# Two causal attentions of a two-block network on one core: the mask written into PSUM by ScalarE instead of added by TensorE

## What is computed

```python
# fox_attention, per block of 128 queries
logits = einsum('bhqd,bhkd->bhqk', qh[:, :, s0:end], kh[:, :, :end])
logits = logits + c[:, :, s0:end, None] - c[:, :, None, :end]
mask = (s0 + arange(Q_BLOCK))[:, None] >= arange(end)[None, :]
p = softmax(where(mask, logits, -inf), axis=-1)
outs.append(einsum('bhqk,bhkd->bhqd', p, vh[:, :, :end]))

# mla_mixer, per block of 128 queries
s = einsum('bqhd,bkhd->bhqk', qn, k_nope) + einsum('bqhr,bkr->bhqk', qp, k_pe)
s = where(k_idx[None, :] <= q_idx[:, None], s * scale, NEG_INF)
p = softmax(s, axis=-1)
```

## Time and profile before

| | before |
|---|---|
| median of three runs | 2364.09 us (2361.83 to 2372.06) |
| profiled execution, its own time | 2368.16 us |
| its span | 2366.2 us |
| PE busy | 2260.8 us (96%), 29050 instructions |
| PEld busy | 2018.5 us (85%) |
| DVE busy | 597.1 us (25%) |
| ACT busy | 474.1 us (20%), 1038 instructions |
| POOL busy | 40.9 us (2%) |
| granted TensorE clock, mean | 0.983 |
| DMA | 522.04 MB, mean 221 GB/s |
| stretch of the fox attention | about 526 to 569 us |
| stretch of the MLA attention | about 923 to 960 us |

### The profile page before, as it was taken

The page is one execution under the profiler, slowest core; times in us unless marked ns, Lnnn a source line. Parts: engine busy times, 40 slices in busy tenths (PEclk is TensorE's granted clock), DMA queues, the critical chain, the costliest instruction groups (busy, mean ns, idle before and its releaser), DMA issues.

```text
span 2366.2 us, 64576 instructions
## 1 busy us (share of the span) xinstructions
PE 2260.8 (96%) x29050; PEld 2018.5 (85%) x29050; DVE 597.1 (25%) x1485; ACT 474.1 (20%) x1038; POOL 40.9 (2%) x31
## 2 busy tenths in 40 slices
PE   7998999899899989999997899999999999999998
PEld 6877888667788866788885789999999999999998
DVE  3414332204333235311359320111111111111111
ACT  3422111213221124201123121111111111111111
POOL 0000000000000000000014100000000000000000
PEclk9999999999999999999998999999999999999999
DMA  7122443140333313233431239999999999999996
GB/s 310 72 116 97 160 160 142 72 159 26 147 138 142 140 66 148 107 115 152 195 125 37 107 130 352 382 354 379 356 387 350 383 345 391 333 396 339 397 357 260
DMA packets 103107, 522.04 MB, mean 221 GB/s; under 512 B 8369, under 2 KB 8498, under 8 KB 95410
## 3 DMA queue, kind: packets, MB, share of 16 engines
q1 hardware_dynamic: 102962, 519.82, 57.3%
HBM read 518.74 MB, written 1.05 MB: 220 GB/s over the span
## 4 chain that ended last, share of the span: by engine, by line
PE 91%; DVE 6%; ACT 1%; issue 1%; DMA 0%; SPq 0%; DVEq 0%; ACTq 0%
PE ps L1479 25%; PE ps L957 18%; PE ps L1493 13%; PE ps L936 10%; PE ps L968 9%; PE ps L1014 3%; PE ps L918 2%; PE ps L1180 1%; PE ps L1466 1%; DVE scr L1971 1%; PE ps L982 1%; PE ps L1437 1%; DVE rstd L1596 1%; PE ps L1123 1%; PE ps L1166 1%
## 5 line engine op out<-in xcount | busy, mean ns | idle before, releaser
L1479 PE MATMUL ps<-scr,slot 128*64 128x96 f32 x14336 | 636.4, 246 | 3.7 <-issue 3.7
L1479 PEld LDWEIGHTS ps<-scr,slot 128*64 128x64 f32 x14336 | 611.3, 137 | 4.6 <-issue 4.6
L957 PE MATMUL ps<-hT,slot 128*128 128x256 f32 x2016 | 445.4, 379 | 0.0
L957 PEld LDWEIGHTS ps<-hT,slot 128*128 128x128 f32 x2016 | 383.0, 190 | 52.1
L1493 PE MATMUL ps<-scr,slot 128*64 128x96 f32 x7168 | 341.4, 247 | 0.2 <-issue 0.2
L1493 PEld LDWEIGHTS ps<-scr,slot 128*64 128x64 f32 x7168 | 313.5, 137 | 24.4 <-issue 24.3
L968 PE MATMUL ps<-scr,slot 128*128 128x256 f32 x1056 | 242.3, 383 | 4.9 <-DVE scr L1806 4.9
L968 PEld LDWEIGHTS ps<-scr,slot 128*128 128x128 f32 x1056 | 202.7, 192 | 34.5 <-DVE scr L1806 6.5
L814 ACT ACTIVATE scr<-ps 128x96 f32<-128x96 f32 x224 | 56.2, 251 | 826.3 <-PE ps L1479 826.3
L2100 DVE TENSOR_TENSOR scr<-scr,ps 128x96 f32<-128x96 f32 x224 | 56.4, 252 | 613.2 <-PE ps L1479 613.2
L936 PE MATMUL ps<-hT,slot 128*128 128x256 f32 x736 | 166.1, 385 | 3.5 <-DVE hT L1583 2.9
(11 more groups left out here) (333 smaller groups left out, 1428.6 us busy)
## 6 DMA issues: line engine op xcount, KB each, us to landing
slot<-in_w_moe SPq DMA_DIRECT2D x224, 1024.0 KB, 7.1
slot<-in_w_moe SPq DMA_DIRECT2D x224, 512.0 KB, 6.9
slot<-in_w_ffn SPq DMA_DIRECT2D x33, 3072.0 KB, 10.1
slot<-in_w_even_in SPq DMA_DIRECT2D x4, 3072.0 KB, 23.0
slot<-in_w_odd_qk SPq DMA_DIRECT2D x2, 3072.0 KB, 10.1
slot<-in_w_s_glu SPq DMA_DIRECT2D x2, 3072.0 KB, 10.6
slot<-in_w_odd_v SPq DMA_DIRECT2D x2, 2048.0 KB, 8.4
slot<-in_w_even_out SPq DMA_DIRECT2D x1, 3072.0 KB, 10.1
```

The source lines that it names most:

```text
L957: m = pe.matmul(pair(f, k), w[:, o:o + P], hT[:, c], start=c == 0, stop=c == KD - 1, skip_group_check=True)
L1479: m = pe.matmul(pair(f, k)[s:s + STRIP, 0:CAP], w[:, o:o + STRIP], xg[e % 2][:, c], start=c == 0, stop=c == KD - 1, skip_group_check=True)
```

## The change

The mask no longer goes onto the scores behind them, but lies in PSUM ahead of them, and the products add onto it.

- GpSimd builds mask3 in SBUF, 384 columns wide: mask, zeros, mask. It does so once, when mixT of the first layer is complete (parts 22 and 23 of the scratch tensor; mag_ moves from there to part 11).
- For pairs 0 and 1 of each attention TensorE writes mask3 into the two banks by one product with the identity per head (start=True), ahead of the head products.
- For pairs 2 to 7 ScalarE copies mask3 into the bank of each head, in biased(p), behind turned(p) and ahead of mixed(p-1); it waits for the exponents of pair p, which read these banks last. TensorE's scores(p+2) waits for biased(p) in place of the exponents.
- All products of scores now have start=False. The mask products behind them are gone, and at["scores"] is incremented by the last product of each head (L1204 in fox, the second L1235 of a head in MLA).

The diff, without the list of semaphores:

```diff
@@ -325,7 +325,8 @@
         mraw = part(0, 6).rearrange("p (a n) -> p a n", a=6)
         mnorm = part(6, 5).rearrange("p (a n) -> p a n", a=5)
         qpe_raw = part(12, 4).rearrange("p (a n) -> p a n", a=4)
-        kpe, cos, sin, ang, turns, red, mag_ = (part(16 + i) for i in range(7))
+        kpe, cos, sin, ang, turns, red, mag_ = (part(i) for i in (16, 17, 18, 19, 20, 21, 11))
+        mask3 = part(22, 2)[:, 0:3 * P]
         posf = scr[0:1, 24 * T:25 * T]
         onesrow = scr[0:1, 25 * T:25 * T + P]
         tmp = part(30, 2).rearrange("p (a n) -> p a n", a=2)
@@ -455,6 +456,10 @@
             pool.affine_select(out=sc, in_=sc, pattern=[[0, 16], [1, CHUNK]], base=0,
                                channel_multiplier=-1, compare_op=ALU.is_ge, fill=0.0
                                ).then_inc(hg["masked"], 1)
+            pool.wait_ge(mix_ready, KD)
+            for b in (0, 2):
+                pool.tensor_copy(mask3[:, b * P:(b + 1) * P], mask).then_inc(at["maskmade"], 1)
+            pool.memset(mask3[:, P:2 * P], 0.0).then_inc(at["maskmade"], 1)
 
             def phase(q):
 
@@ -604,6 +609,13 @@
                                    bias=stat[:, h, 4:5], scale=scale_of[kind],
                                    accum_out=stat[:, h, 6:7]).then_inc(at["exp"], 1)
 
+                def biased(p):
+
+                    act.wait_ge(at["exp"], n0 + 2 * p + 2)
+                    for h in (2 * p, 2 * p + 1):
+                        act.activation(ps[:, 4 + h % 4, 0:3 * P], mask3, ACT.Copy
+                                       ).then_inc(at["biased"], 1)
+
                 def turned(p):
 
                     act.wait_ge(at["pturned"], n0 + 2 * p + 1)
@@ -616,6 +628,7 @@
                     act.wait_ge(at["out"], p0 + p + 1)
                     act.activation(mixT[:, p], ps[:, p % 2, 0:T], ACT.Copy).then_inc(mix_ready, 1)
 
+                act.wait_ge(at["maskmade"], 3)
                 exponents(0)
                 exponents(1)
                 for p in range(HEADS // 2):
@@ -623,6 +636,8 @@
                         exponents(2 * p + 2)
                         exponents(2 * p + 3)
                     turned(p)
+                    if p + 2 < HEADS // 2:
+                        biased(p)
                     if p:
                         mixed(p - 1)
                 mixed(HEADS // 2 - 1)
@@ -1111,18 +1126,18 @@
             def attention(kind, products):
                 n0 = at0[kind]
                 p0 = n0 // 2
+                b0 = 0 if kind == "fox" else HEADS - 4
 
                 def scores(p):
 
+                    heads = (2 * p, 2 * p + 1)
                     if p >= 2:
-                        pe.wait_ge(at["exp"], n0 + 2 * p - 2)
-                    heads = (2 * p, 2 * p + 1)
+                        pe.wait_ge(at["biased"], b0 + 2 * p - 2)
+                    else:
+                        for h in heads:
+                            pe.matmul(ps[:, 4 + h % 4, 0:3 * P], ident, mask3, start=True, stop=False,
+                                      skip_group_check=True)
                     products(heads)
-                    for h in heads:
-                        for c in (0, 2 * P):
-                            m = pe.matmul(ps[:, 4 + h % 4, c:c + P], ident, mask, start=False,
-                                          stop=True, skip_group_check=True)
-                        m.then_inc(at["scores"], 1)
 
                 def turn(h):
                     pe.wait_ge(at["prob"], n0 + h + 1)
@@ -1148,6 +1163,7 @@
                     m.then_inc(at["out"], 1)
 
                 pe.wait_ge(at["vtaken"], 4 if kind == "fox" else 8)
+                pe.wait_ge(at["maskmade"], 3)
                 scores(0)
                 for p in range(HEADS // 2):
                     if p + 1 < HEADS // 2:
@@ -1165,7 +1181,7 @@
                         r = HD * (h % 2)
                         pe.matmul(ps[:, 4 + h % 4, qb * P:(2 * qb + 1) * P],
                                   proj[r:r + HD, h // 2, qb * P:(qb + 1) * P],
-                                  proj[r:r + HD, 8 + h // 2, 0:(qb + 1) * P], start=qb == 0,
+                                  proj[r:r + HD, 8 + h // 2, 0:(qb + 1) * P], start=False,
                                   stop=False, skip_group_check=True)
 
             def values(phase, src, k, n0):
@@ -1202,7 +1218,8 @@
                     for h in heads:
                         one = cst[0:HEADS, CST["ident"] + h:CST["ident"] + h + 1]
                         pe.matmul(ps[:, 4 + h % 4, 0:3 * P], one.to_broadcast([HEADS, P]), negc,
-                                  start=False, stop=False, skip_group_check=True)
+                                  start=False, stop=True, skip_group_check=True
+                                  ).then_inc(at["scores"], 1)
 
                 attention("fox", products)
 
@@ -1232,10 +1249,12 @@
                     for qb in range(2):
                         for h in heads:
                             r = ROPE * (h % 4)
-                            pe.matmul(ps[:, 4 + h % 4, qb * P:(2 * qb + 1) * P],
+                            m = pe.matmul(ps[:, 4 + h % 4, qb * P:(2 * qb + 1) * P],
                                       proj[r:r + ROPE, 16 + h // 4, qb * P:(qb + 1) * P],
-                                      kpe[r:r + ROPE, 0:(qb + 1) * P], start=False, stop=False,
+                                      kpe[r:r + ROPE, 0:(qb + 1) * P], start=False, stop=qb == 1,
                                       skip_group_check=True)
+                            if qb:
+                                m.then_inc(at["scores"], 1)
 
                 attention("mla", products)
                 linear("mla_o", mixT, mix_ready, mix0["mla_o"])
```

More of the change, by code:

```diff
@@ L288, in build_program @@
         at = {n: sem("at_" + n) for n in (
-            "flog", "fbias", "logsig", "c", "vtile", "vtaken", "scores", "max", "exp", "prob",
+            "flog", "fbias", "maskmade", "biased", "logsig", "c", "vtile", "vtaken", "scores", "max", "exp", "prob",
             "pturned", "eventaken", "oddtaken", "out", "posrow", "poscol", "reduced", "trig", "turned", "roped")}
```

## The result

| | before | changed |
|---|---|---|
| median | 2366.7 us (2361.83 to 2372.06, 4 runs) | 2403.99 us (2402.16 to 2406.17, 4 runs) |
| ratio | | 1.0155, 95% interval 1.0139 to 1.0172 |
| span of the profiled execution | 2366.2 us | 2402.4 us |
| granted TensorE clock, mean | 0.983 | 0.970 |
| PE busy | 2260.8 us | 2278.0 us |

A forecast was written before the change was run, and what follows sets the result against it. TensorE, never waiting in steady head pairs, was taken as the bound of both attentions; the new wait added 5.55 us in fox and 9.05 in MLA, +14.6 on the 2364.1 median, forecasting 2379 us, range 2368 to 2392.

The forecast's parts named there:

- The wait: Both attentions: scores wait on a chain from the previous pair's scores; 5.71 us per fox pair, 5.59 per MLA pair.
- The mask copies: ScalarE, pairs 2 to 7 of each attention: two 384-column copies take 0.90 us together, bounds 0.60 to 1.04.
- Masks on TensorE for pairs 0 and 1: Start of each attention: two 384-column products per pair take 1.48 us, 5.9 us over four pairs.
- Pair 1 to pair 2: Stretch between these pairs' starts on TensorE: +3.11 us in fox, +3.60 us in MLA.
- the rest at nothing: Building the mask, waits for it, the score semaphore, mag_'s new place and the weights were all taken to cost nothing.
- The clock: Rival in both attentions: granted clock falls in TensorE's new pauses, +10 us, 2389 us; chance 0.17.
- The sum: Both attentions at full clock: fox +5.55 us and MLA +9.05 us, together +14.6 us.
- fox's five turns: Fox, pair 2 to pair 7: five turns at 5.71 us instead of 5.03, +3.40 us.
- MLA's five turns: MLA, pair 2 to pair 7: five turns at 5.59 us instead of 4.41, +5.90 us.
- MLA's end: Behind the start of MLA's pair 7: its maximum comes 1.62 us after the start instead of 2.46, -0.84 us.
- up to +20 us: Under the skill's clock rule, every pair of both attentions would start at the low clock, costing up to this much.
- TensorE stays the bound, and the change pays: Rival in both attentions: masks lie ready in PSUM when TensorE comes, -11.5 us, 2353 us; chance 0.04.

The follow-up runs named there:

- Filled pauses: Changed kernel with dummy TensorE products in its new pauses (4 per fox pair, 5 per MLA pair, 4 more in the first pair); 2385.22 us, ratio 1.0084.
- the wait alone: Kernel before, masks still on TensorE, no mask copies; scores of pair p wait for ScalarE's copy of pair p-2's transposed block; 2388.61 us, ratio 1.0095.
- the swapped order: Changed kernel with dummy products in its pauses and ScalarE's output copy put ahead of the two mask copies; 2385.78 us, ratio 1.0084.
- the run with the moved wait: Changed kernel with ScalarE's wait for the mask table moved from the head of each attention to its first mask copy; 2406.58 us, ratio 1.0164.

## Why the prediction was wrong

- **The wait.** Right, and at its size. TensorE's scores of a pair wait for a chain that begins with the pair before. Its turn was put at 5.71 and 5.59 us and measured at 5.79 and 5.80 at full clock. VectorE's maximum, ScalarE's exponents, L612's copy and the masks stand in it as forecast. Filled pauses, the wait alone and the swapped order all moved with it.
- **The mask copies.** Right: put at 0.40 + 0.50, bounded by 0.60 to 1.04 for two. In the changed kernel one takes 0.500 us and two 0.91. Their cost was not the matter: one pair earlier the same 24 copies hold up no fox pair, and MLA pairs are shorter than before as well.
- **Masks on TensorE for pairs 0 and 1.** Right: pair 0 to pair 1 took 0.36 and 0.37 us longer, forecast 0.39.
- **Pair 1 to pair 2.** Put at +3.11 and +3.60, measured 8.19 - 4.08 = +4.11 and 8.83 - 3.73 = +5.10. Of the 2.5 us between, the run with the moved wait gives 2.2 to the table load (8.19 - 7.27 and 8.83 - 7.54), which the step "the rest at nothing" had missed: it took the wait for the mask table for one that is over long before, which it is, and did not see that it displaces another wait. Moving the wait showed it.
- **The clock. This is the step that failed.** The sum left the granted clock at 1.00 and gave its fall a chance of 0.17, because the pairs' products are larger than those of S5 and TensorE stays busy for 3.3 us or more of each turn. Neither kept the clock up: it was 0.50 in most pairs, and that cost 17 to 19 us, as the run with filled pauses shows. Of the 38.4 us in the two attentions the sum had 14.6. It missed 9.4 us in fox's five turns (37.97 us against 5 x 5.71), 5.2 behind the start of fox's last pair, where the low clock lasted to 588 us, and 6.5 in MLA's five turns (34.47 against 5 x 5.59). These 21.1 us, of which some 1.5 are the turns' small error at full clock, with the 2.5 us above and 0.2 at MLA's end, are the whole miss.
- **The price in that rival.** Too low as well (2389 us), by two arguments. One was "TensorE would have 2 x 3.94 us of work and no pause left; so I count every second of the 12 turns": a pause was left, and most pairs ran so. The other, "At half the clock a turn gets longer by TensorE's part, 1.6 to 1.7 us", held for MLA (7.25 - 5.80 = 1.45) but not for fox (8.19 - 5.79 = 2.40). The chain of waits of the changed kernel, from one fox pair at half clock to the next, shows the longer way:

```profile
566.13 2.85 PE ps L1220 x4
568.98 1.48 PE ps L1159 x8
570.46 0.85 PE ps L1147 x3
571.31 0.02 issue
571.33 0.03 ACT scr L624
571.36 0.36 issue
571.72 0.91 ACT ps L616 x2
572.62 0.04 issue
572.67 1.66 PE ps L1182 x8
```

At half clock fox's loop no longer runs over the maximum and the exponents. It runs over all of TensorE's work up to the transposes of one head (L1147), which ScalarE's L624 waits for, and from there over the masks to the next scores: 1.66 + 2.85 + 1.48 + 0.85 and 1.4 for ScalarE and the semaphores. TensorE is busy for 7.46 of 8.19 us and yet the pause of 0.73 us stays, and with it, in most pairs, the clock of 0.50. The prediction took a nearly full TensorE for one whose clock comes back.
- **The rule of the Trainium skill** on the clock ("TensorE: Matmul & The Clock Gate", section "HAM oscillation — how this bites in real kernels") was the better guide here: bursts separated by waits can start slow. The traces agree, at 0.67 and 0.74 of the clock in the mean over the two attentions; the clock fell in the first pauses, of 3.3 and 3.1 us, and again in pauses of 1.8 and 2.4 us. The prediction's "up to +20 us" for this case was close to the 17 to 19 us that the clock cost.
- **"TensorE stays the bound, and the change pays".** Wrong for this change, and right for its neighbour: with the copies one pair earlier it is what happens, 9 us for 11.5 that this rival priced (TensorE is the bound in fox, VectorE nearly so in MLA). It decided where it was said to, at the place of the copies in ScalarE's queue.

## What to carry to other kernels

Before moving work to an idle engine, read where in that engine's queue it lands: a short instruction behind the wait of the *next* step turns a double buffer into a single one, and one step earlier the same instruction held nothing up here. When a change makes pauses on TensorE, price them twice, once as time and once with every product around them at half clock, and walk the loop again at that clock, since it can close over another path. And a wait added ahead of an instruction can push that instruction's own wait onto a table load before it.

## What the hardware showed that was not expected

- The granted clock stayed at 0.50 over pairs in which TensorE was busy for 7.46 of 8.19 us, with pauses of 0.73 us.
- Dummy products make a waiting kernel faster: by 17 to 19 us here.
- ScalarE writing 384 columns from SBUF to PSUM takes 0.500 us, reading them from PSUM to SBUF 0.487 (the median of L612; 0.49 in the earlier trace rows). Source and destination both differ, so this says nothing on PSUM as a destination alone. Line L616 of the changed kernel, all its instructions and who waited for them:

```profile
L616 ACT ACTIVATE ps<-scr x24: 486/500/502, 533.7 to 987.6; 128x384 f32<-128x384 f32 x24
...
  PE ps L1182: 17.8, 12
```

Twelve waits, one for each of the twelve pairs that ScalarE masks.
